# Two moves around the attention loop: the modulation products at other pairs, and eight of twelve bias pieces on GpSimd

## The reference, cut to what matters

```python
sh1, sc1, g1, sh2, sc2, g2 = silu(cond) @ w_ada + b_ada      # w_ada: 1024 x 6144
h = rms_norm(x, norm1_w) * (1 + sc1) + sh1
q, k, v, gu, gv = split(h @ w_in)
a = attend(q, k, v)            # 8 heads x 64; latent rows get a learned position bias
sg = spatial_gating(gu, gv)
x = x + g1 * (concat([a, sg]) @ w_out)
h2 = rms_norm(x, norm2_w) * (1 + sc2) + sh2
x = x + g2 * moe(h2)           # 16 experts, top 2 of one group
```

## Time and profile before

| | us |
|---|---|
| median of 3 runs | 623.93 |
| the 3 runs | 623.8, 623.93, 627.05 |
| the profiled execution | 627.05 |
| its span, first to last instruction | 625.3 |
| TensorE busy | 535.3 (86%) |
| VectorE busy | 412.3 (66%) |
| ScalarE busy | 280.1 (45%) |
| GpSimd busy | 188.4 (30%) |

### The profile page before, as it was taken

One profiled execution on the slowest core, in us unless ns is written; L12 is line 12 of the kernel. 1 busy time (PEld: TensorE's weight loads), 2 busy tenths in 40 slices (PEclk: granted clock), 3 DMA queues, 4 the chain that ended last, 5 costly groups with the idle time before them and its releaser, 6 DMA issues.

```text
span 625.3 us, 8731 instructions
## 1 busy us (share of the span) xinstructions
PE 535.3 (86%) x2930; PEld 420.8 (67%) x2930; DVE 412.3 (66%) x606; ACT 280.1 (45%) x408; POOL 188.4 (30%) x209
## 2 busy tenths in 40 slices
PE   3889997899999888997899994589999999999800
PEld 3337885699899536755688883377888888888600
DVE  3417556577610748957543558769989989899338
ACT  5308114141221215655510242238888888888300
POOL 2031132301100230000300002434788777874210
PEclk9878999899999989999799997689999999999955
DMA  9992030213261819307275334299596599997667
GB/s 327 387 315 90 0 136 17 90 46 134 88 232 38 291 45 381 146 2 271 76 294 210 160 120 183 85 351 344 198 376 252 178 362 384 372 363 274 244 241 275
DMA packets 41888, 130.98 MB, mean 209 GB/s; under 512 B 6237, under 2 KB 6253, under 8 KB 35585
## 3 DMA queue, kind: packets, MB, share of 16 engines
q1 hardware_dynamic: 32176, 109.62, 47.1%
q0 software_dynamic: 8688, 20.42, 9.3%
q10 hardware_dynamic: 992, 0.55, 0.3%
HBM read 121.35 MB, written 18.38 MB: 223 GB/s over the span
## 4 chain that ended last, share of the span: by engine, by line
PE 71%; DVE 14%; DMA 6%; ACT 3%; issue 3%; POOL 1%; ACTq 1%; SPq 0%; DVEq 0%; POOLq 0%
PE bank L1394 18%; PE bank L1396 17%; PE bank L1395 17%; PE bank L1390 3%; PE bank L1669 3%; DMA big<-w_ada 2%; PE bank L1512 2%; PE bank L1554 2%; PE bank L1602 1%; PE bank L1536 1%; DVE big_r L939 1%; PE bank L1431 1%; DMA big<-w_out 1%; PE bank L1526 1%; PE bank L1404 1%
## 5 line engine op out<-in xcount | busy, mean ns | idle before, releaser
L1394 PE MATMUL bank<-big_r 128*128 128x512 f32 (+1 forms) x264 | 100.5, 381 | 0.0
L1163 DVE TENSOR_TENSOR big_r<-big,big_r 128x2048 fp32r<-128x2048 f32 x38 | 87.3, 2296 | 5.9 <-ACT big_r L809 5.7
L809 ACT ACTIVATE big_r<-big 128x2048 fp32r (+1 forms) x38 | 72.9, 1918 | 30.2 <-issue 27.2
L1395 PE MATMUL bank<-big_r 128*128 128x512 f32 x200 | 78.7, 393 | 0.0
L1396 PE MATMUL bank<-big_r 128*128 128x512 f32 (+1 forms) x176 | 63.7, 362 | 0.0
L1396 PE MATMUL bank<-big_r,hu_r 128*128 128x512 f32 x160 | 62.8, 393 | 0.0
L1394 PEld LDWEIGHTS bank<-big_r 128*128 128x128 f32 x264 | 53.9, 204 | 7.2 <-issue 0.9
L557 POOL TENSOR_TENSOR small<-small 128x8 f32<-128x8 f32 (+1 forms) x15 | 21.5, 1433 | 89.3 <-DVE small L997 55.3
L1395 PEld LDWEIGHTS bank<-big_r 128*128 128x128 f32 x200 | 41.9, 210 | 6.7 <-issue 0.4
L939 DVE TENSOR_TENSOR big_r<-big,big_r 128x1024 fp32r<-128x1024 f32 x28 | 33.0, 1220 | 12.3 <-ACT big_r L697 12.3
L634 POOL COPY small<-small 128x1 uint32 x19 | 32.3, 1700 | 25.8 <-ACT rs L864 18.1
(11 more groups left out here) (268 smaller groups left out, 1191.4 us busy)
## 6 DMA issues: line engine op xcount, KB each, us to landing
big<-w SPq DMA_DIRECT2D x32, 1024.0 KB
big<-w_ada SPq DMA_DIRECT2D x12, 2048.0 KB, 15.1
hu<-w SPq DMA_DIRECT2D x16, 1024.0 KB
big<-w_in SPq DMA_DIRECT2D x5, 2048.0 KB, 9.3
big<-slot_out SPq DMA_DIRECT2D x10, 512.0 KB, 7.9
big<-w_out SPq DMA_DIRECT2D x2, 2048.0 KB, 10.5
x_rows<-big SPq DMA_DIRECT2D x5, 512.0 KB, 2.6
h_rows<-vr SPq DMA_DIRECT2D x5, 512.0 KB, 3.0
```

The lines of the kernel that those rows point to most:

```text
L809: nc.scalar.activation(w13_hi[p][:, v, :], w13_raw(v, par), ACT.Copy).then_inc(w13_hi_ready, 1)
L1163: V.tensor_tensor(w13_lo[p][:, v, :], w13_raw(v, par), w13_hi[p][:, v, :].bitcast(F32), ALU.subtract).then_inc(w13_lo_ready, 1)
L1394: T.matmul(out, lhs[0], rhs[0], start=start, stop=False)
L1395: T.matmul(out, lhs[0], rhs[1], start=False, stop=False)
```

## The change

The two groups of modulation products move. Group 0 goes from the pairs 0, 1, 2 (3, 3, 2 row blocks) to the pairs 1 and 2 (4 and 4). Group 1 goes from the pairs 12, 13, 14 to 8, 9, 10 (3, 3, 2 in both). `ada_group(1)` follows from pair 14 to pair 10, and the waits of `ada_part` and `sums_T` on counters are set to match. The bias pieces 4 to 11 go from VectorE to GpSimd, which makes them behind its last small transfer and counts them in a new semaphore, `bias_pool`; what waited for these pieces waits for that. VectorE keeps the pieces 0 to 3 at the pairs 0 and 1. Nothing that is computed changes.

```diff
-        ada_at = {m: (g, ks) for g, first in enumerate((0, 3 * PPT)) for m, ks in (
-            (first, range(0, 3)), (first + 1, range(3, 6)), (first + 2, range(6, KD)))}
-        ada_ends = {2: 0, 3 * PPT + 2: 1}
+        ada_at = {1: (0, range(0, 4)), 2: (0, range(4, KD)), 2 * PPT: (1, range(0, 3)), 2 * PPT + 1: (1, range(3, 6)),
+                  2 * PPT + 2: (1, range(6, KD))}
+        ada_ends = {2: 0, 2 * PPT + 2: 1}
...
-        bias_at = {0: (0, 1), 1: (2, 3), 2: (4, 5), 3: (6, 7), 7: (8,), 8: (9,), 9: (10,), 10: (11,)}
+        bias_at = {0: (0, 1), 1: (2, 3)}
...
+            pool.wait_ge(slab_in, 16)
+            for i in range(4, 2 * len(bias_pieces)):
+                nc.gpsimd.tensor_tensor(*bias_parts(i), ALU.add).then_inc(bias_pool, 1)
 
             pool.wait_ge(row_out, 16 * 8)
...
-                    act.wait_ge(bias_ready, 2 * len(bias_pieces))
+                    act.wait_ge(bias_ready, 4)
+                    act.wait_ge(bias_pool, 8)
...
-                dve.wait_ge(bias_ready, 4 if g == 0 else 2 * len(bias_pieces))
+                dve.wait_ge(bias_ready, 4)
+                if g:
+                    dve.wait_ge(bias_pool, 8)
...
-                    dve.wait_ge(bias_ready, {1: 4, 4: 12}.get(t, 8))
+                    dve.wait_ge(bias_ready, 4)
+                if t >= 2:
+                    dve.wait_ge(bias_pool, 8 if t == 4 else 4)
...
-                    pe.wait_ge(sT_copied, 3)
+                    pe.wait_ge(sT_copied, 2)
...
-                pe.wait_ge(rows_ready, 1 if t < 3 else 2)
+                pe.wait_ge(rows_ready, 1 if t < 2 else 2)
```

More of the change, by code:

```diff
@@ L243, in build @@
         ring_in = [sem(f"ring_in{s}") for s in range(RING + 1)]
-        zero_ready, bias_ready = sem("zero_ready"), sem("bias_ready")
+        zero_ready, bias_ready, bias_pool = sem("zero_ready"), sem("bias_ready"), sem("bias_pool")
         fold_ready, ada1_done, bias_zeroed, rows_ready = [sem(n) for n in (
@@ L348, in build, with bias_parts @@
         PPT = HEADS // 2
-        ada_at = {m: (g, ks) for g, first in enumerate((0, 3 * PPT)) for m, ks in (
-            (first, range(0, 3)), (first + 1, range(3, 6)), (first + 2, range(6, KD)))}
-        ada_ends = {2: 0, 3 * PPT + 2: 1}
+        ada_at = {1: (0, range(0, 4)), 2: (0, range(4, KD)), 2 * PPT: (1, range(0, 3)), 2 * PPT + 1: (1, range(3, 6)),
+                  2 * PPT + 2: (1, range(6, KD))}
+        ada_ends = {2: 0, 2 * PPT + 2: 1}
         bias_pieces = ((LEFT_EDGE, 2, "from"), (LEFT_EDGE + 1, 4, "right"), (INNER, 1, "upper"), (INNER + 1, 3, "lower"),
                        (RIGHT_EDGE, 0, "left"), (RIGHT_EDGE + 1, 2, "upto"))
-        bias_at = {0: (0, 1), 1: (2, 3), 2: (4, 5), 3: (6, 7), 7: (8,), 8: (9,), 9: (10,), 10: (11,)}
+        bias_at = {0: (0, 1), 1: (2, 3)}
+        def bias_parts(i):
+            piece, rel, name = bias_pieces[i // 2]
+            odd = i % 2
+            keys = bass.AP(slab.tensor, slab.offset + HALF_W * rel + odd * RPB_W,
+                           [slab.ap[0], slab.ap[1], (1, COLS), (2 * RPB_W, GRID_H // 2)])
+            return (bm[:, :, piece, :].rearrange("p h (c a b) -> p h c a b", a=2, c=COLS)[:, :, :, odd], keys,
+                    masks[name].rearrange("p (c a b) -> p c a b", a=2, c=COLS)[:, :, odd].unsqueeze(1).to_broadcast(
+                        (P, HEADS, COLS, GRID_H // 2)))
         def bias_of(t):
@@ L1096, in bias_piece @@
             def bias_piece(i):
-                piece, rel, name = bias_pieces[i // 2]
-                odd = i % 2
                 if i == 0:
@@ L1102, in bias_piece @@
                     dve.wait_ge(sgu_out, TILES)
-                keys = bass.AP(slab.tensor, slab.offset + HALF_W * rel + odd * RPB_W,
-                               [slab.ap[0], slab.ap[1], (1, COLS), (2 * RPB_W, GRID_H // 2)])
-                V.tensor_tensor(
-                    bm[:, :, piece, :].rearrange("p h (c a b) -> p h c a b", a=2, c=COLS)[:, :, :, odd], keys,
-                    masks[name].rearrange("p (c a b) -> p c a b", a=2, c=COLS)[:, :, odd].unsqueeze(1).to_broadcast(
-                        (P, HEADS, COLS, GRID_H // 2)), ALU.add).then_inc(bias_ready, 1)
+                V.tensor_tensor(*bias_parts(i), ALU.add).then_inc(bias_ready, 1)
             def copy_pT(m):
```

## The result

The changed kernel takes 633.16 us (median of 4 runs, 630.69 to 636.23) where the kernel before, timed beside it, has 625.49 (4 runs, 623.8 to 629.66): a ratio of 1.0112, 95% interval 1.0072 to 1.0151. It is slower. The prediction had the direction right and the size too small: 628.1 was forecast, and the range ended at 631.2. A cost of 4.5 to 7.4 us is in both intervals.

What follows compares the result with a forecast made beforehand. TensorE's attention loop, with its stops for a chunk, row sums and VectorE's copies, sets when the output products start. Terms +5.2 (pair 8), -0.5 (pairs 8 to 16) and -0.5 (w_out) gave +4.2 on 623.9: 628.1 us, range 624.6 to 631.2.

Steps and rivals of the forecast that it cites:

- Group 0: Start of the loop: in two pieces with TensorE at full clock, group 0 ends at 228.5, 3.5 us earlier.
- rival 1: At 220 the clock falls as before: group 0 ends at 230.8, sum +6.5, 630.4 us; chance 0.2.
- Bias pieces off VectorE: Ahead of `ada_group(0)`: the row at 234.89 moves 4.6 us forward, pairs 4 to 7 about 5 us early.
- Bias pieces on GpSimd: Eight pieces of 1.8 us from 224.7 to 239, hidden up to 4 us a piece.
- Weights not there at pair 8: Group 1's chunks land at 254.7; TensorE stops 6.1 us, clock falls, values of pair 8 start 5.2 us later.
- a wait below 3 us: At pair 8: sign that the forecast is wrong; about 6 us idle, ended by the w_ada transfer, was its sign of right.
- Pairs 8 to 16: Middle of the loop: 34.4 us in place of 34.9, -0.5 us, with about 3.9 us idle in pairs 11 to 15.
- w_out earlier: Before pair 16: w_out is issued near 270, not 284, so its 0.49 us wait goes, -0.5 us.
- Rival 4: GpSimd too slow: costs only above 6 us a piece; at 7 us, 4 us more, 632; chance 0.03.
- Rival 2: Pairs 17 to 19: the half clock at the loop's end goes, 2.5 us less, 625.6 us; chance 0.15.
- Rival 3: Pair 8: weights land sooner behind group 0's end, 621.6 at 22 us, 617.9 from 20 us down; chance 0.05.
- rival 5: Whole kernel: groups simply trade places and the change is worth nothing, 623.9 within a microsecond; chance 0.12.

Runs made afterwards that it cites:

- the end edited: VectorE's four rounding pieces of w_out one pair later: the kernel before with it 619.92 us (ratio 0.9899), the changed kernel with it 626.09 us (0.9991).
- groups_only: The changed kernel with all twelve bias pieces on VectorE at their old pairs, so only the groups move; 632.71 us, ratio 1.0115 to the kernel before.
- paced_g0: The changed kernel with group 1 back at pairs 12 to 14 and each GpSimd piece released behind one pair's maxima; 624.68 us, ratio 0.9966.
- g0_only: The kernel before with only group 0 moved to pairs 1 and 2, group 1 at 12 to 14, bias pieces on VectorE; 624.32 us, ratio 0.9985.
- g1_at_9: The changed kernel with all bias pieces on VectorE and group 1 at pairs 9 and 10, four row blocks each; 629.09 us, ratio 1.0025.
- pool_only: The kernel before with groups unmoved and only bias pieces 4 to 11 on GpSimd, in one burst; 635.41 us, ratio 1.0144.
- before_again: The kernel before, run once more without an edit; 623.62 us, ratio 0.9978.
- issues_between: Groups 0 at pairs 1 and 2, 1 at 12 to 14; GpSimd puts a small transfer behind each bias piece instead of waiting; 637.16 us, ratio 1.0134.

## Why the prediction was right or wrong, point by point

- **Group 0.** Right in the number, not in how it comes about. It ends 13.4, 13.9 and 13.6 us into the loop in the three traces of the changed kernel (with the end edited or not); 228.5 - 215.41 = 13.1 was forecast, from a stop of 1.5 us and products at full clock. None of the three has that stop. Their first 16 products take 5.30, 5.83 and 5.91 us without idle time, where the next 16 take 3.64, since the granted clock is at half (1.2 GHz) there (0.50 in 220 to 221 us of the first trace), though the only stop near it is the 1.15 us ahead of the loop. So rival 1's clock came without rival 1's price, and that the end agrees is luck. In groups_only it went as forecast: a stop of 1.46 us, then full clock, an end at 13.8.
- **Bias pieces off VectorE** (the row sums 4.6 us earlier, pairs 4 to 7 five). Wrong in the changed kernel, where the row at 240.45 is late. Without the hold, the values of pair 4 come 3 to 4 us earlier than in before (24.3 and 23.0), but the pieces have no part in it: they stand at 19.9 in paced_g0 with the pieces on GpSimd and at 19.7, 20.2 and 20.4 in g0_only, g1_at_9 and groups_only with the pieces on VectorE. The stop for the row sums is gone in all four. The gain is that of group 0.
- **Bias pieces on GpSimd, "hidden up to 4 us a piece".** This is the step that failed. The duration was fair (1.5 us, 1.8 taken). What was priced was who waits for the pieces, not whom they stop: the effect on VectorE was put at nothing. The runs show VectorE's negation held to the end of the burst, 10.00, 9.49 and 9.79 us in the three traces of the changed kernel, and TensorE stopped 7.24, 6.74 and 7.03 us for the row sums, where the forecast had no stop. In pool_only this term alone costs 8 to 9 us. The sum came near only because the delay priced at pair 8 lies behind it and disappears when TensorE comes late. That is luck: the prediction worked out no such hold.
- **Weights not there at pair 8.** Right as a mechanism, shown by groups_only, g1_at_9 and g0_only, but not seen in the changed kernel, which has no wait at pair 8, where the prediction named a wait below 3 us as its sign of being wrong. There the stop of 7.24 us for the held VectorE takes the place of a stop of 5.2 and half clock behind it. Over three traces each (with the end edited or not) the values of pair 8 moved from 37.2 to 43.9, **+6.7**; +5.2 was forecast. This term is too small by 1.5.
- **Pairs 8 to 16.** -1.1 in all traces, -0.5 forecast. Right in sign: the idle time ahead of the values of the pairs 12, 14 and 16 was 2.9 us in all (1.10, 1.09, 0.69), where about 3.9 was forecast (its five terms give 3.8).
- **w_out earlier.** -0.5 forecast. ScalarE no longer waits for it, but the ends of the loop vary by 1.4 us by themselves, and with the end edited they are equal: nothing shows.
- **The sum.** The loops differ by 4.9 us (two traces each) and 6.4 us (the end edited), in place of 4.2.
- **The base.** The difference was put on a median of three, 623.93. The kernel before had medians of 625.5 to 627.5 in the later comparisons (623.62 as before_again), and its profiled execution had 627.05. About 2 of the 5 us between 628.1 and 633.16 are this, 1 to 2 the sum; the rest is no more than the scatter of the four runs (630.69 to 636.23).
- **Rival 4 (GpSimd too slow)** set its price by the duration of a piece, with no effect below 6 us. It is the nearest to what happened, and had the wrong mechanism. Rival 2's full clock came in part in the first trace (1.00 from 299 to 308, about 0.55 behind the stop of 3.66 us) and not in the second (0.50 from 300 to 308). The stretch to the output is 17.24 and 17.58 us for 18.18 and 17.09 before, so it is not worth 2.5 us. Rival 3 falls, since the fourth chunk landed 27.6 us behind group 0 in groups_only and 28.1 in g1_at_9, and rival 5 since the change costs time. Rival 1's fall of the clock came in all three traces of the changed kernel, and in one of the three of the kernel before.

## What to carry to other kernels

Before work is given to an idle engine, ask not only who waits for its result but what that engine shares with the busy one while it runs: here a two-column negation of 0.17 us took 10. Long GpSimd work beside VectorE cost nothing that the time shows in single pieces released at a known point (paced_g0, 624.68 us, beside g0_only, 624.32), and 9 us as a burst (pool_only). And when two delays lie ahead of the same row, removing one may show nothing: take each away alone and both together before calling either harmless.

## What the runs showed of the hardware

- VectorE's copies and tensor_scalar operations from SBUF to SBUF were held until GpSimd's back-to-back burst of two-input additions ended (10.00, 9.49, 9.79, 10.38 and 3.71 us for negations of 0.17, 4.91 for a copy of 0.43), within 0.3 us of the end of the burst. Copies, reductions and additions with an operand in PSUM, and a reciprocal, were not. Gaps of 0.5 us in the burst let VectorE in at two places and not at two others.
- Two bias pieces of VectorE, with both inputs in SBUF, took 3.25 us beside GpSimd's pieces (once, in issues_between) and 2.03 otherwise.
- The clock behind the same stop differs between executions of the same kernel: at half speed (1.2 GHz) behind 2.61 us, at full (2.4 GHz) behind 3.05 us. In the changed kernel it was at half with no stop but 1.15 us ahead of it. An argument from the length of one stop, as the prediction made, is worth a range and not a value; here 1.7 us.
